# Hybrid decoder trunk: the first half of x loaded in three pieces, the norm weights first, fewer idle turns

## The chip, the cores and the metric

The kernel runs on one core of a Trainium2 chip. The metric is the device time of one execution in microseconds (us); lower is better. Times are medians of several executions.

## The reference

Two layers of a decoder trunk on 256 tokens of width 1024, in float32. Each layer computes:

```python
h = rms_norm(x, g_mix[l])
parts = split(h @ w_in[l])                  # one projection, 10656 columns
# A: sliding-window attention, B: latent attention, C: dilated attention in 3 groups,
# M: cross-attention into rms_norm(mem)
y = einsum('bsnc,ncd->bsnd', o, w_branch[l])
x = x + einsum('bsnd,de->bse', sigmoid(gate_pre + b_gate[l]) * y, w_out[l])
u = rms_norm(x, g_mlp[l]) @ w_up[l]
x = x + square(relu(u)) @ w_down[l]
```

## The kernel before, in words

All products are made in three passes of float32r: each operand is split in a rounded part ("hi") and the rest ("lo"), and TensorE adds hi x hi, hi x lo and lo x hi (L1524 to L1526). 200 MB of weights are streamed once. SyncE (SP) walks the list of weight units in order (L929): a unit is one or two blocks of 128 rows by 512 columns, in a ring of four places, `raw`. Before it issues unit u it waits until unit u-4 has been split, that is until VectorE has made its lo part (`lo_split`). ScalarE (ACT) makes the hi part of a unit (L1043), VectorE (DVE) the lo part (L1230), and TensorE then does the unit's "chunks", six matmuls for each block of 128 rows.

The activations need a preparation. x lies with the tokens on the partitions and has to be turned: TensorE transposes a block of 128 columns for both token tiles (a "turn", L1555, two transposes a column block), ACT evicts it from PSUM with the column's norm weight as scale into `h_hi` (L1126), DVE makes `h_lo` (L1379). The norm weights `g_mix` of layer 0 come by their own small DMA, are turned by TensorE (`gains_first`, L1493) and kept by ACT (`keep_first`, L1031); the evictions wait for them. A first product needs unit 0's lo part and the `h_lo` of column block 0.

The order on every engine is made in Python before the program is written. `plan` makes a list of items with modelled costs, needs, an `order` number and sometimes an earliest time `since`. `arrange` places them: again and again it takes the engine that can begin soonest, and on it, among the items that can begin within a small look-ahead (0.1 us on TensorE, 0.25 on ACT and DVE, none for DMA), the one with the lowest order. For DMA items it adds up modelled transfer times from 2.2 us on at 300 GB/s; an item that needs a transfer becomes ready 1.2 us after it. The item `gains_first` has `since=4.0`. The costs are 0.276 us for a turn of one block, 0.15 for `gains_first`, 0.25 for `keep_first`, 0.49 for an eviction of one block, and 0.62 and 0.69 for a one-block unit's hi and lo part. The order numbers at the start are -9.0, -7.64, -6.28, -4.92 for units 0 to 3 (loads, hi and lo), -20 to -17 for the turns of column blocks 0 to 3, three less for their evictions, and 0 for `gains_first` and `keep_first`.

The real transfers are written by hand beside that. SP issues units 0 to 4, then after unit 4 the positions and the rotary frequencies (L934, L936; many descriptors of 4 and 192 bytes), then unit 5 and behind it the second half of x (L932). ACT issues columns 0 to 255 of x (L1021), the norm weights (L1022) and columns 256 to 511 (L1023), and then begins its list. `mem` is loaded by ACT after the hi part of unit 5.

TensorE begins with 14 idle turns of the identity (L1478), has 8 more ahead of the first chunk, and otherwise follows the plan. The first squares of x (`square`) wait for all pieces of x.

Of the kernel before, what the change touches and what calls it, by code (L numbers as in the profile page):

```python
# [7 lines left out]
P = 128  # L8
# [11 lines left out]
DC = D // P  # L20
# [31 lines left out]
MASK = {("A", 0): (0, P), ("A", 1): (P, S), ("B", 0): (0, P), ("B", 1): (P + S, S),  # L52
        ("C", 0): (P + 2 * S, C_BLOCKS * P), ("C", 1): (P + 2 * S + C_BLOCKS * P, C_BLOCKS * P)}
MASK_W = P + 2 * S + 2 * C_BLOCKS * P
STAT = {"h": ("h", 0), "y": ("r", 0), "lat": ("r", 0), "lat3": ("r", 3), "m": ("r", 0), "r0": ("r", 0), "r1": ("r", 4)}
LOADS = 7
ALL_LOADS = 9 * DEPTH - 1
# [95 lines left out]
def plan():  # L153
# [8 lines left out]
    def item(kind, engine, cost, needs, order=None, chain=None, since=0.0, **a):  # L162
        it = Item(kind, engine, cost, axis[0] if order is None else order,
                  [b if isinstance(b, tuple) else (b, None) for b in needs if b is not None], a, since)
        chain = kind if chain is None else chain
        if chain:
            if chain in last_of:
                it.needs.append((last_of[chain], None))
            last_of[chain] = it
        items.append(it)  # L170
        return it
# [325 lines left out]
    masks = item("masks", "DVE", 2.0, [], order=15.0, since=15.4)  # L497
    selects = item("selects", "POOL", 5.0, [masks], order=25.0)

    for k, (size, order) in enumerate(((256, -8.95), (256, -7.6), (512, -0.7))):  # L500
        x_loads.append(item("load_x", "DMA", 256 * size * 4 / 300e3, [], order=order, part=k))
    gains_first = item("gains_first", "PE", 0.15, [], since=4.0)
    gains_first = item("keep_first", "ACT", 0.25, [gains_first])
    gains_turn = item("gains_turn", "PE", 0.15, [], since=20.0, order=20.0)
# [5 lines left out]
    for l in range(DEPTH):  # L510

        def x_turns(c0, c1, dest, gain, came, jobs_needed, order=None):
            for c, m in [(c, 1) for c in range(c0, half)] * (not jobs_needed) + [(c, 2) for c in range(max(c0, 0 if jobs_needed else half), c1, 2)]:
                turn(("x", jobs_needed), came if jobs_needed else [(x_loads[min(c // 2, 2)], 1.2)], c, m, P, dest, "split", gain, l,
                     order=order if jobs_needed or c >= half else c - 20.0)

        if l == 0:
# [197 lines left out]
def hybrid_block(nc, x, mem, positions, inv_freq, g_mix, w_in, b_gate, a_qn, a_kn, a_sink, b_qa_norm, b_kva_norm,  # L715
# [34 lines left out]
    with ExitStack() as ctx:  # L750
# [3 lines left out]
        def sem(name):  # L754
            return ctx.enter_context(nc.semaphore(name))
# [103 lines left out]
        bias_landed = [sem("bias_landed%d" % i) for i in range(2)]  # L859
        mem_landed = [sem("mem_landed%d" % i) for i in range(TT)]  # L860
        gains_landed = sem("gains_landed")
        x_landed, freq_landed = [sem("x_landed%d" % i) for i in range(3)], sem("freq_landed")
        seeded = sem("seeded")
        pool_const, dve_const, ident_ready = sem("pool_const"), sem("dve_const"), sem("ident_ready")
        angle_ready, trig_ready, table_ready = sem("angle_ready"), sem("trig_ready"), sem("table_ready")
# [52 lines left out]

        x_rows = x.rearrange("b (t p) d -> p (b t) d", p=P)

        @block.sync
        def _(sp):
            at_u = {}
            for u, w in enumerate(units):
                if u >= RAW:
                    sp.wait_ge(lo_split, u - RAW + 1)
                l, r0 = w["l"], w["l"] * rows[w["w"]] + w["row"]
                src = flat[w["w"]][r0:r0 + w["kn"] * P, w["col"]:w["col"] + w["cn"]]
                sp.dma_start(unit_in(raw, raw_up, u), src.rearrange("(k p) n -> p k n", p=P))\  # L929
                    .then_inc(raw_landed[u % RAW], 16)  # L930
                if u == 5:
                    sp.dma_start(xs[:, :, NW:D], x_rows[:, :, NW:D]).then_inc(x_landed[2], 16)  # L932
                if u == 4:
                    sp.dma_start(pos_in.bitcast(I32), positions.rearrange("b (t p) -> p (b t)", p=P),  # L934
                                 allow_slow_non_contiguous=True).then_inc(freq_landed, 16)
                    sp.dma_start(inv_in, inv_freq.broadcast_to([P, FREQ])).then_inc(freq_landed, 16)  # L936
                if l == 0 and u >= 9 or l and units[u - 1]["l"] < l:
                    at_u[l] = min(at_u.get(l, u), u)
                if l in at_u:
                    if l and u == at_u[l]:  # L940
                        sp.wait_ge(gain_table, count["table"] // DEPTH * l)
                    for dst, src in row_gains(l)[2 * (u - at_u[l]):2 * (u - at_u[l]) + 2]:
                        sp.dma_start(dst, src.broadcast_to([P, src.shape[1]]), allow_slow_non_contiguous=True).then_inc(gains_landed, 16)
            to = out.rearrange("b (t p) d -> p (b t) d", p=P)
            first, second = jobs[-2], jobs[-1]
            sp.wait_ge(set_free[first.j % 2], set_value(first))
            sp.dma_start(to[:, :, 0:NW], xs[:, :, 0:NW]).then_inc(stored, 16)
            sp.wait_ge(half_added, 1)
            sp.dma_start(to[:, 0, NW:D], xs[:, 0, NW:D]).then_inc(stored, 16)
            sp.wait_ge(set_free[second.j % 2], set_value(second))  # L950
            sp.dma_start(to[:, 1, NW:D], xs[:, 1, NW:D]).then_inc(stored, 16)
            sp.wait_ge(stored, 48)
# [65 lines left out]

        @block.scalar
        def _(act):  # L1020
            act.dma_start(xs[:, :, 0:2 * P], x_rows[:, :, 0:2 * P]).then_inc(x_landed[0], 16)  # L1021
            act.dma_start(g_first, g_mix[0].rearrange("(c p) -> c p", p=P)).then_inc(g_first_landed, 16)  # L1022
            act.dma_start(xs[:, :, 2 * P:NW], x_rows[:, :, 2 * P:NW]).then_inc(x_landed[1], 16)  # L1023
            act.wait_ge(seeded, 1)
            nc.scalar.activation(nothing[:], no_mask[:], ACT.Sin)
            gained = False
            for it in placed["ACT"]:
# [19 lines left out]
                elif it.kind == "square":  # L1047
# [3 lines left out]
                    if src == "D":  # L1051
                        job, seg = a["job"], a["segs"][0]
                        tile = home_of(homes[a["tok"]])
                        act.wait_ge(set_free[job.j % 2], set_value(job))
                        if seg.get("st") == 2 * HD:
                            to = sq[:, 0:TT * seg["n"] * HD].rearrange("p (t h d) -> p t h d", t=TT, d=HD)
                            of = tile[:, :, 0:4 * B_W].rearrange("p t (h d) -> p t h d", d=B_W)[:, :, :, 0:HD]
                        else:
                            w = job.cn
                            if not seg.get("st"):  # L1060
                                w = max(g["col"] + g["n"] * g["d"] for g in a["segs"])
                            to = sq[:, 0:TT * w].rearrange("p (t c) -> p t c", t=TT)
                            of = tile[:, :, 0:w]
                        nc.scalar.activation(to, of, ACT.Square).then_inc(squares, 1)
                    else:
                        if a["q"] >= STATS:
                            act.wait_ge(root_ready, a["q"] - STATS + 1)
                        if src == "x":
                            for c in range(3):
                                act.wait_ge(x_landed[c], 16)  # L1070
                            for job in a["jobs"]:
                                act.wait_ge(set_free[job.j % 2], set_value(job))
                            of = xs[:, a["tt"]]
                        else:
                            act.wait_ge(mem_landed[a["tt"]], 16 * (a["l"] + 1))
                            of = mem_in[:, a["tt"]]
                        nc.scalar.activation(sq[:], of, ACT.Square, accum_out=sums[:, slot, 0:1]).then_inc(squares, 1)
# [396 lines left out]
        def _(pe):  # L1474
            def idle_turns(n):

                for _ in range(n):
                    nc.tensor.transpose(ps_d[:, 1, 0, 0:P], ident[:], ident[:])  # L1478

            pe.wait_ge(ident_ready, 1)  # L1480
            idle_turns(14)
            for it in placed["PE"]:
                a = it.a
                if it is first_chunk:
                    idle_turns(8)
                for b, closes, count_freed in a["prior"]:
                    if closes is not None and closes.kind == "mask":
                        pe.wait_ge(masked, closes.a["e"] + 1)
# [39 lines left out]
                elif it.kind == "turn":  # L1528
                    (src, i), b, m, wd = a["source"], it.banks[0], a["m"], a["width"]
                    if src == "tok":  # L1530
                        if a["ready"] is not None:
                            pe.wait_ge(tok_ready, a["ready"] + 1)
                        else:
                            pe.wait_ge(scaled, a["scaled"] + 1)
                    elif src == "x":
                        if not i:
                            pe.wait_ge(x_landed[min(a["c"] // 2, 2)], 16)
                        for job in i:
                            pe.wait_ge(set_free[job.j % 2], set_value(job))
                        if a["piece"]:  # L1540
                            pe.wait_ge(part_added, a["piece"])
                    elif src == "mem":
                        for tt in range(TT):
                            pe.wait_ge(mem_landed[tt], 16 * (a["l"] + 1))
                    elif src == "Y":
                        pe.wait_ge(y_added, a["mixed"].a["added"])
# [96 lines left out]
```

## Time and profile before

| | us |
|---|---|
| median of 3 runs | 1180.99 (1180.57 to 1181.22) |
| the profiled execution, its own time | 1182.1 |
| its span in the trace | 1180.3 |
| first real product starts (in the span) | 7.39 |
| PE busy | 1174.4 |
| DVE busy | 822.2 |
| ACT busy | 698.0 |

The profile counts time from the start of the span. A busy time of TensorE holds the modelled ends of overlapping matmuls, so in a dense stretch it is the starts of successive matmuls that tell the pace. The change touches only the first microseconds; the rows shown below are from there and from the places that lie behind them.

### The profile page before, as it was taken

Reading aid. Unit: us, or ns where it says so; the run is one execution under the profiler, and the core shown is the slowest. Engines: PE = TensorE matmul, PEld = TensorE weight load, DVE = VectorE, ACT = ScalarE, POOL = GpSimd, SP = SyncE. Lnnn points to the kernel's source line nnn. Section 1 sums busy time; section 2 is a strip of 40 time slices with the busy share of each in tenths; the row PEclk is TensorE's granted clock in tenths of the full one; section 3 lists DMA queues with packets and bytes.
Section 4 is the critical chain, followed back from the end, with each engine's and each line's share of the span. In section 5 each row is a group of like instructions: output and inputs, shape, how many; then the busy total and the mean of one; then the engine's idle time right before and its main releaser. Section 6 shows DMA issues by size and latency. Waiting matters only on the chain.

```text
span 1180.3 us, 18491 instructions
## 1 busy us (share of the span) xinstructions
PE 1174.4 (100%) x6808; PEld 1007.7 (85%) x6808; DVE 822.2 (70%) x1319; ACT 698.0 (59%) x1114; POOL 139.9 (12%) x129
## 2 busy tenths in 40 slices
PE   9999999999999999999999999999999999999998
PEld 7888888888888899999888888888888888999897
DVE  6787989987766764454567788989876767555544
ACT  6667866655544474555476677666654445655453
POOL 6211422300000000000021123232000000000000
PEclk9999999999999999999999999999999999999999
DMA  8655446554576556565756554465545665665653
GB/s 280 197 157 157 127 140 197 160 171 129 163 211 203 182 174 190 186 190 186 205 153 200 145 155 126 140 192 168 161 139 165 179 198 177 179 194 182 194 182 105
DMA packets 127878, 204.75 MB, mean 173 GB/s; under 512 B 9206, under 2 KB 50736, under 8 KB 127792
## 3 DMA queue, kind: packets, MB, share of 16 engines
q1 hardware_dynamic: 122528, 194.64, 54.7%
q10 hardware_dynamic: 4720, 8.92, 2.5%
q8 instruction: 56, 0.92, 0.3%
q14 instruction: 30, 0.25, 0.1%
q0 software_dynamic: 544, 0.03, 0.0%
HBM read 200.41 MB, written 1.05 MB: 171 GB/s over the span
## 4 chain that ended last, share of the span: by engine, by line
PE 95%; DMA 2%; DVE 2%; ACT 1%; POOL 1%; issue 1%; ACTq 0%; POOLq 0%; DVEq 0%
PE ps_d L1524 23%; PE ps_d L1526 22%; PE ps_d L1525 22%; PE ps_b L1515 5%; PE ps_b L1517 5%; PE ps_b L1516 5%; PE ps_b L1579 4%; PE ps_b L1555 3%; PE ps_b L1613 3%; PE ps_b L1587 2%; DMA raw<-in_m_w_kv_dram 1%; DMA raw<-in_w_in_dram 1%; DVE w_lo L1230 1%; PE ps_d L1478 0%; POOL root L984 0%
## 5 line engine op out<-in xcount | busy, mean ns | idle before, releaser
L1230 DVE TENSOR_TENSOR w_lo<-raw,w_hi 128x1024 fp32r<-128x1024 f32 (+3 forms) x382 | 450.6, 1185 | 265.5 <-ACT w_hi L1043 264.2
L1043 ACT ACTIVATE w_hi<-raw 128x1024 fp32r<-128x1024 f32 (+3 forms) x382 | 391.8, 1027 | 371.1 <-PE ps_d L1526 282.1
L1524 PE MATMUL ps_d<-w_hi,h_hi 128*128 128x512 f32 (+3 forms) x704 | 279.5, 397 | 0.0
L1526 PE MATMUL ps_d<-w_hi,h_lo 128*128 128x512 f32 (+3 forms) x704 | 267.3, 380 | 0.0
L1525 PE MATMUL ps_d<-w_lo,h_hi 128*128 128x512 f32 (+3 forms) x704 | 266.9, 379 | 0.0
L1524 PE MATMUL ps_d<-w_hi,r_hi 128*128 128x512 f32 (+1 forms) x552 | 217.5, 394 | 0.0
L1526 PE MATMUL ps_d<-w_hi,r_lo 128*128 128x512 f32 (+1 forms) x552 | 214.1, 388 | 0.0
L1525 PE MATMUL ps_d<-w_lo,r_hi 128*128 128x512 f32 (+1 forms) x552 | 214.0, 388 | 0.0
L1526 PEld LDWEIGHTS ps_d<-w_hi,h_lo 128*128 128x128 f32 x704 | 132.3, 188 | 25.1
L1524 PEld LDWEIGHTS ps_d<-w_hi,h_hi 128*128 128x128 f32 x704 | 132.5, 188 | 24.8 <-issue 2.9
L1525 PEld LDWEIGHTS ps_d<-w_lo,h_hi 128*128 128x128 f32 x704 | 132.8, 189 | 20.5
L1515 PE MATMUL ps_b<-h_hi,w_hi 128*128 128x256 f32 x512 | 145.6, 284 | 0.0
L1517 PE MATMUL ps_b<-h_hi,w_lo 128*128 128x256 f32 x512 | 144.9, 283 | 0.0
L1516 PE MATMUL ps_b<-h_lo,w_hi 128*128 128x256 f32 x512 | 144.9, 283 | 0.0
L1524 PEld LDWEIGHTS ps_d<-w_hi,r_hi 128*128 128x128 f32 x552 | 103.8, 188 | 21.0 <-ACT q_c L1095 0.6
L1526 PEld LDWEIGHTS ps_d<-w_hi,r_lo 128*128 128x128 f32 x552 | 103.6, 188 | 21.0
L1525 PEld LDWEIGHTS ps_d<-w_lo,r_hi 128*128 128x128 f32 x552 | 103.8, 188 | 19.1
L984 POOL TENSOR_TENSOR root<-sums,power 128x16 f32<-128x16 f32 (+3 forms) x32 | 82.4, 2576 | 271.6 <-DVE sums L1308 259.4
L1515 PEld LDWEIGHTS ps_b<-h_hi,w_hi 128*128 128x128 f32 x512 | 98.2, 192 | 1.3 <-issue 0.5
L1516 PEld LDWEIGHTS ps_b<-h_lo,w_hi 128*128 128x128 f32 x512 | 98.3, 192 | 0.5
L1517 PEld LDWEIGHTS ps_b<-h_hi,w_lo 128*128 128x128 f32 x512 | 98.2, 192 | 0.0
L984 POOL TENSOR_TENSOR factor_mlp<-sums,inverse 128x1 f32<-128x1 f32 x4 | 2.2, 558 | 371.7 <-DVE sums L1317 371.7
(172 smaller groups left out, 1158.6 us busy)
## 6 DMA issues: line engine op xcount, KB each, us to landing
raw<-in_w_in_dram SPq DMA_DIRECT2D x150, 512.0 KB, 3.7
raw<-in_w_up_dram SPq DMA_DIRECT2D x64, 512.0 KB, 3.7
raw<-in_w_down_dram SPq DMA_DIRECT2D x64, 512.0 KB, 3.7
raw<-in_w_branch_dram SPq DMA_DIRECT2D x32, 512.0 KB, 3.8
raw<-in_m_w_kv_dram SPq DMA_DIRECT2D x16, 512.0 KB, 5.8
raw<-in_w_out_dram SPq DMA_DIRECT2D x16, 512.0 KB, 4.2
early<-in_b_gate_dram ACTq DMA_DIRECT2D x16, 256.0 KB, 4.2
raw<-in_w_in_dram SPq DMA_DIRECT2D x12, 256.0 KB, 3.5
```

Source lines behind the costliest of these rows:

```text
L984: nc.gpsimd.tensor_tensor(to, sums[:, slot, 0:w], by, ALU.pow).then_inc(root_ready, 1)
L1043: nc.scalar.activation(unit_in(w_hi, hi_up, u), unit_in(raw, raw_up, u), ACT.Copy).then_inc(hi_split, 1)
L1230: nc.vector.tensor_tensor(unit_in(w_lo, lo_up, u), unit_in(raw, raw_up, u), unit_in(w_hi, hi_up, u).bitcast(F32), ALU.subtract).then_inc(l ...
L1515: nc.tensor.matmul(o, wh, hi[:, a["c"]], start=a["first"], stop=False)
L1516: nc.tensor.matmul(o, wh, lo[:, a["c"]], start=False, stop=False)
L1517: last = nc.tensor.matmul(o, wl, hi[:, a["c"]], start=False, stop=a["last"])
L1524: nc.tensor.matmul(o, hi[:, a["c"], cut], wh, start=a["first"], stop=False)
L1525: nc.tensor.matmul(o, hi[:, a["c"], cut], wl, start=False, stop=False)
L1526: last = nc.tensor.matmul(o, lo[:, a["c"], cut], wh, start=False, stop=a["last"])
L1555: last = nc.tensor.transpose(ps_b[0:wd, b, k * P:(k + 1) * P], v, ident[:])
L1579: last = nc.tensor.matmul(ps_b[:, b, c:c + wide], q, k, start=True, stop=True)
L1613: last = nc.tensor.matmul(ps_b[r0:r0 + d, b, c:c + P], v[:, vh * d:(vh + 1) * d], turned_prob_of(st)[:, k * P:(k + 1) * P], start=k == 0, ...
```

## The change

Columns 0 to 511 of x come in three pieces (one column block, one, and two) instead of two of 256 columns. The first of them is issued by ACT, now behind the norm weights; the second and third by SP, behind units 0 and 1. The second half of x stays behind unit 5. Each turn waits for the piece that its block is in; the squares wait for four. The planner gets four x transfers, with orders -9.05, -8.95, -7.6, -0.7. The idle turns go from 14 to 10 at the beginning, and from 8 to 5 ahead of the first chunk.

```diff
+X_LOADS = ((0, 1), (1, 2), (2, 4), (4, DC))
+X_LOAD = [k for k, (c0, c1) in enumerate(X_LOADS) for _ in range(c0, c1)]
...
-    for k, (size, order) in enumerate(((256, -8.95), (256, -7.6), (512, -0.7))):
-        x_loads.append(item("load_x", "DMA", 256 * size * 4 / 300e3, [], order=order, part=k))
+    for k, ((c0, c1), order) in enumerate(zip(X_LOADS, (-9.05, -8.95, -7.6, -0.7))):
+        x_loads.append(item("load_x", "DMA", S * (c1 - c0) * P * 4 / 300e3, [], order=order, part=k))
...
-                turn(("x", jobs_needed), came if jobs_needed else [(x_loads[min(c // 2, 2)], 1.2)], ...
+                turn(("x", jobs_needed), came if jobs_needed else [(x_loads[X_LOAD[c]], 1.2)], ...
...
+        def load_x(eng, k):
+            cut = slice(X_LOADS[k][0] * P, X_LOADS[k][1] * P)
+            eng.dma_start(xs[:, :, cut], x_rows[:, :, cut]).then_inc(x_landed[k], 16)
...
-                if u == 5:
-                    sp.dma_start(xs[:, :, NW:D], x_rows[:, :, NW:D]).then_inc(x_landed[2], 16)
+                if u in (0, 1, 5):
+                    load_x(sp, {0: 1, 1: 2, 5: 3}[u])
...
-            act.dma_start(xs[:, :, 0:2 * P], x_rows[:, :, 0:2 * P]).then_inc(x_landed[0], 16)
             act.dma_start(g_first, g_mix[0].rearrange("(c p) -> c p", p=P)).then_inc(g_first_landed, 16)
-            act.dma_start(xs[:, :, 2 * P:NW], x_rows[:, :, 2 * P:NW]).then_inc(x_landed[1], 16)
+            load_x(act, 0)
...
-            idle_turns(14)
+            idle_turns(10)
...
-                    idle_turns(8)
+                    idle_turns(5)
...
-                            pe.wait_ge(x_landed[min(a["c"] // 2, 2)], 16)
+                            pe.wait_ge(x_landed[X_LOAD[a["c"]]], 16)
```

## Rows read from the trace of the kernel before

**Rows 1.** Busy time by engine, from the page: us, share, instructions.

```profile
PE 1174.4 (100%) x6808; PEld 1007.7 (85%) x6808; DVE 822.2 (70%) x1319; ACT 698.0 (59%) x1114; POOL 139.9 (12%) x129
```

**Rows 2.** Waits of TensorE, whole span: us in total, times, longest.

```profile
PE ps_d L1478 <- POOL ident L962: 1.8, 1, 1.8
PE ps_b L1555 <- DVE tok L1360: 0.8, 1, 0.8
```

**Rows 3.** Timeline, TensorE: start us, length us, engine line operation.

```profile
1.78 3.25 PE L1478 MATMUL ps_d<-ident 128*128 128x128 f32 x14 [1.78 <-POOL ident L962]
...
5.06 0.27 PE L1493 MATMUL ps_d<-ident,early 8*128 8x8 f32 x1
...
5.26 1.11 PE L1555 MATMUL ps_b<-ident,xs 128*128 128x128 f32 x4
...
6.17 1.47 PE L1478 MATMUL ps_d<-ident 128*128 128x128 f32 x8
...
7.39 0.48 PE L1524 MATMUL ps_d<-w_hi,h_hi 128*128 128x512 f32 x1
...
14.55 0.39 PE L1526 MATMUL ps_d<-w_hi,h_lo 128*128 128x512 f32 x1
...
14.94 1.07 PE L1555 MATMUL ps_b<-ident,xs 128*128 128x128 f32 x8
```

**Rows 4.** Timeline, ScalarE, ahead of the first product and at 21 us.

```profile
4.34 0.63 ACT L1043 ACTIVATE w_hi<-raw 128x512 fp32r<-128x512 f32 x1 [0.51 <-DMA raw<-in_w_in_dram]
...
5.37 0.18 ACT L1031 ACTIVATE g_all<-ps_d 128x8 f32<-128x8 f32 x1 [0.40 <-PE ps_d L1493]
...
5.99 0.90 ACT L1126 ACTIVATE h_hi<-ps_b,g_all 128x256 fp32r<-128x256 f32 x2 [0.44 <-PE ps_b L1555]
...
21.65 1.06 ACT L1043 ACTIVATE w_hi<-raw 128x1024 fp32r<-128x1024 f32 x1 [1.89 <-DMA raw<-in_w_in_dram]
```

**Rows 5.** Timeline, VectorE, ahead of the first product.

```profile
5.00 0.69 DVE L1230 TENSOR_TENSOR w_lo<-raw,w_hi 128x512 fp32r<-128x512 f32 x1 [5.00 <-ACT w_hi L1043]
...
6.50 0.91 DVE L1379 SCALAR_TENSOR_TENSOR h_lo<-ps_b,g_all,h_hi 128x256 fp32r<-128x256 f32 x2 [0.80 <-ACT h_hi L1126]
...
7.44 1.29 DVE L1230 TENSOR_TENSOR w_lo<-raw,w_hi 128x512 fp32r<-128x512 f32 x2
```

**Rows 6.** Timeline, DMA issues on the queues of SP and ACT.

```profile
0.74 5.36 SPq L929 DMA_DIRECT2D raw<-in_w_in_dram  x5
0.75 0.48 ACTq L1021 DMA_DIRECT2D xs<-in_x_dram  x1
...
1.26 0.61 ACTq L1022 DMA_DIRECT2D early<-in_g_mix_dram  x1
...
6.66 0.47 SPq L936 DMA_DIRECT2D early<-in_inv_freq_dram  x1
...
8.16 0.37 SPq L929 DMA_DIRECT2D raw<-in_w_in_dram  x1
...
8.57 0.47 SPq L932 DMA_DIRECT2D xs<-in_x_dram  x1
```

**Rows 7.** DMA issues of 0 to 0.9 us: KB, us to landing.

```profile
xs<-in_x_dram ACTq DMA_DIRECT2D x1, 256.0 KB, 4.3
```

**Rows 8.** DMA issues of 8.5 to 9 us.

```profile
xs<-in_x_dram SPq DMA_DIRECT2D x1, 512.0 KB, 6.2
```

**Rows 9.** DMA issues of the whole span, from the page: median us to landing.

```profile
raw<-in_w_in_dram SPq DMA_DIRECT2D x150, 512.0 KB, 3.7
```

**Rows 10.** Busy time by stretch; the last three numbers: granted clock, DMA share, GB/s.

```profile
4.00:5.00 1.00, 1.00 (x5) 0.63 (x3) 0.00 (x0) 0.63 (x1) 1.00 (x3) 1.00 1.07 398
...
9.00:10.00 1.00, 1.00 (x9) 0.87 (x8) 0.21 (x1) 0.72 (x2) 1.00 (x3) 1.00 0.27 45
...
12.00:14.00 2.00, 2.00 (x10) 1.65 (x10) 0.85 (x1) 0.56 (x1) 0.18 (x1) 1.00 1.06 400
```

**Rows 11.** The chain that ended last, in order of time: start us, us, what.

```profile
12.88 8.75 DMA raw<-in_w_in_dram
```

More of the change, by code:

```diff
@@ L513, in x_turns @@
             for c, m in [(c, 1) for c in range(c0, half)] * (not jobs_needed) + [(c, 2) for c in range(max(c0, 0 if jobs_needed else half), c1, 2)]:
-                turn(("x", jobs_needed), came if jobs_needed else [(x_loads[min(c // 2, 2)], 1.2)], c, m, P, dest, "split", gain, l,
+                turn(("x", jobs_needed), came if jobs_needed else [(x_loads[X_LOAD[c]], 1.2)], c, m, P, dest, "split", gain, l,
                      order=order if jobs_needed or c >= half else c - 20.0)
@@ L861, in hybrid_block @@
         gains_landed = sem("gains_landed")
-        x_landed, freq_landed = [sem("x_landed%d" % i) for i in range(3)], sem("freq_landed")
+        x_landed, freq_landed = [sem("x_landed%d" % i) for i in range(len(X_LOADS))], sem("freq_landed")
         seeded = sem("seeded")
@@ L1068, in _ @@
                         if src == "x":
-                            for c in range(3):
-                                act.wait_ge(x_landed[c], 16)
+                            for landed in x_landed:
+                                act.wait_ge(landed, 16)
                             for job in a["jobs"]:
```

## The prediction

> **What bounds the kernel now.** I read four views, in this order. The page's busy times: TensorE is busy for 1174.4 of the 1180.3 us of the span [rows 1], so the end moves only by what TensorE does more or less, or waits more or less. TensorE's waits: beside the wait for the identity there is one named stall, 0.8 us, for a rotated token tile [rows 2]; it lies at 62.5 to 63.7 us. The timeline of the first 15 us: real work starts at 7.39 and is dense up to 14.55, where the turns of the second half of x follow at 14.94 instead of about 0.23 later; that is a small stall of 0.16 us, and x's second half, issued at 8.57, lands 6.2 us after, at 14.8 [rows 3, 6, 8]. The chain that ended last: it does not run over the first product alone but, from 12.88, over a weight transfer of 8.75 us [rows 11], which ACT awaited for 1.89 us up to 21.65 [rows 4], and from there over ACT and DVE work to the stall at 62.5. So two things reach the end: TensorE's own start, less what the stall at 62.5 swallows (up to 0.9 us), and the time at which the transfers after 8 us land. The second is the stronger, because it moves the stall itself.
>
> **The order that the planner gives.** I followed its rules with the new numbers; I take only the order from them, not a time. The modelled transfers are: piece 0 to 2.64 us, unit 0 to 3.51 (3.07 before), piece 1 to 3.95, and from unit 1 on as before. Block 0's turn can begin at 3.84, before `gains_first` with its `since` of 4.0, so TensorE now has turn 0, `gains_first`, turn 1. `keep_first` is ready at 4.41 and unit 0's hi part at 4.71, out of the look-ahead of 0.25; then block 0's eviction (4.66, order -23) goes ahead of the hi part too. ACT's order was hi 0, keep, evict 0, evict 1; it becomes keep, evict 0, **hi 0**, evict 1. DVE's was lo 0, h_lo 0, h_lo 1, lo 1; it becomes h_lo 0, lo 0, h_lo 1, lo 1. From unit 2's lo part on the modelled times fall together within 0.03 us, and the rest of the order stays.
>
> **Piece 0 and the norm weights.** The old first piece was issued at 0.75 and landed 4.3 later, at 5.05 [rows 6, 7]; the norm weights were there for the turn at 5.06 [rows 3]. Piece 0 is now issued behind the norm weights, whose issue takes 0.61, so at about 1.37 [rows 6]. Ahead of it stand unit 0 and piece 1, and pieces 0 and 1 together are the 256 KB of the old first piece. I therefore let it land when the old one did plus 0.1 for rows half as long: T = 5.15. Lower bound: half of 256 KB is saved at 398 GB/s [rows 10], 0.33, so 4.7. Upper bound: the old 4.3 from the new issue, 5.7. The norm weights land earlier, but nothing uses that, since their turn now stands behind block 0's.
>
> The Trainium skill ("DMA: Bandwidth & Descriptors", section "Anatomy of one DMA", measured on GpSimd's path) puts a DMA at 2.0 us and its bytes over 436 GB/s; by it 128 KB less would save 0.3 us, and the first product would be late by about 0.2 instead of the 0.5 below. The trace's 4.3 us for 256 KB is far over the 2.6 us of that rule, so it is the transfers ahead, not the size, that this landing waits for.
>
> **From T to the first product.** Two transposes at 0.23 (3.25 us / 14 [rows 3]): 0.46. Norm weights turned and kept: 5.06 to 5.37+0.18 was 0.49 [rows 3, 4]. Eviction of block 0: 0.90 / 2 = 0.45. Hi part of unit 0: 0.63 [rows 4]. Lo part: 0.69 and 0.03 of hand-over [rows 5]. Sum 2.75, so lo 0 ends at 5.15 + 2.75 = 7.90, and it was over at 5.69. The first product starts at 7.9 instead of 7.39: **+0.5 us**. Before, hi 0 and lo 0 lay under the wait for x (4.34 to 5.69); now they are in the line behind it. Bounds from T: +0.1 to +1.1.
>
> **Idle turns.** Ten end at about 1.8 + 2.3 = 4.1, ahead of T. The five behind turn 1 run from about 6.3 to 7.4, under the ACT and DVE work. So the seven that go, 7 x 0.23 = 1.6 us, give 0: the wait behind them is what is late. If they had been in the way they would be worth up to 0.4 (before, `h_lo` of block 0 was ready near 7.0 and the product waited for the idle turns until 7.39 [rows 3, 5]); that is the bound below zero. A cost above zero is the clock rival.
>
> **SP's queue, the main term.** SP issues unit 4 when lo 0 is done. That was 6.10 - 0.38 = 5.72 [rows 5, 6]; it will be 7.95, **+2.2**, and the positions and frequencies behind it are as much later. Unit 5 needs lo 1: 7.90 + h_lo 1 (0.45) + 0.65 = 9.0, but SP itself is busy with the frequencies until 6.66 + 0.47 + 2.2 = 9.35. Unit 5 goes at 9.35 instead of 8.16, and the second half of x at 9.75 instead of 8.57: **+1.2**. The two issues added ahead (pieces 1 and 2, some 0.47 each) push units 1 to 3 by up to 0.9, into time in which the DMA engines have work anyway. With its old 6.2 us the second half of x lands at 16.0. TensorE would be there at 14.94 + 0.5 - 0.16 = 15.3 and waits for it. So everything behind is **1.2 us** later, not 0.5. Unit 4 (about 12.2 with its old flight, hi and lo part 1.06 + 1.23 behind it) would be ready at 14.5, against a TensorE that wants it at about 13.9: 0.6 us, inside the same wait.
>
> Does the rest follow? The DMA engines are full from 12 us on (400 GB/s) and nearly idle between 9 and 10 (45 GB/s) [rows 10]; the full stretch starts with unit 5 and x and has to carry the same bytes, so the unit that ACT awaited until 21.65 is 1.2 later too, and `mem`, which is issued behind unit 5's hi part. The stall at 62.5 then moves with it. Upper bound of the term: the idle dip comes from the frequencies' small descriptors, and these are 2.2 later; if unit 5 keeps its distance from them, the term is 2.2. Lower bound: with less queued ahead unit 5 flies in 3.7 [rows 9] and x's 512 KB follow 1.3 behind it (at 400 GB/s), so x lands at 14.4, no later than before, and the term is 0.
>
> **Sum.** +1.2 us (0 to 2.2). The profiled execution would have 1182.1 + 1.2 = 1183.3 as its own time (span 1181.5). It was 1.1 above the median; on the median the forecast is 1180.99 + 1.2 = **1182.2**. A difference within 0.2% (2.36 us) can't be told from no change here.
>
> **Rivals.**
> Not slower, "x's second half is no later": by the lower bound above, the dip at 9 to 10 us closes and the flight of x is at most 5.0 us. TensorE's 0.3 us delay is swallowed at 62.5. Time 1180.5 to 1181.2. For it: the dip is real idle time. Against it: the descriptors that made it are still ahead of unit 5. It decides from a flight of 5.0 us down.
> Slower, "the frequencies set it": term 2.2, time 1183.2. For it: unit 5 was issued at 8.16 and the engines were still idle between 9 and 10.
> Slower still, "the clock rises later": the idle turns ran at 0.23 us each and the later turns of x at 1.07 / 8 = 0.13 [rows 3], so TensorE left the 1.2 GHz level during the eight idle turns, although the column of the granted clock shows 1.00 there. The new order leaves it without work from 4.1 to 5.15 and from 7.4 to 7.9. If it therefore stays at 1.2 GHz for two chunks (12 products of 0.23 more each) that is 2.8 us, of which the wait for x covers 0.7: 1182.2 + 2.1 = 1184.3. The Trainium skill ("TensorE: Matmul & The Clock Gate", section "What's actually happening") states that the slow clock is the default and activity releases it, at a moment that varies from run to run; it speaks for this rival, and no row here shows a rise after such a gap.
> Faster, "the order stays as it was": if my reading of the planner fails and hi 0 keeps its place, the first product comes up to 0.5 earlier, at 6.9, but the second half of x is not earlier: 1180.6 to 1181.0.
>
> **Chances.** Forecast 0.45, x no later 0.20, frequencies 0.18, clock 0.10, old order 0.07. The forecast's own range is 1181.5 to 1182.9. The range for all, leaving out most of the clock case and the low edge: 1180.1 to 1184.0. Faster by over 0.2% (below 1178.6) fits none of the cases: 0.04 for what I have not seen. Slower by over 0.2% (above 1183.35): most of the clock case and the edge of the frequencies case, 0.13. Within: 0.83.
>
> **What would show it.** In the changed kernel's timeline: TensorE with two turns of x, L1493, two turns; ACT with L1031 and one eviction ahead of the first L1043; the first L1230 ending near 7.9; unit 4 issued near 7.95 and the second half of x near 9.75; its turns near 16.1; the stall at 62.5 still there, and its end near 64.9. I am wrong if the first L1043 still comes first, if x's second half lands before 15 us, or if the products behind the first stand 0.43 apart.

## The result, and the profile after

| | before | changed | |
|---|---|---|---|
| median of 20 runs, us | 1181.04 | 1183.34 | ratio 1.0019 (1.0012 to 1.0026) |
| lowest to highest | 1180.57 to 1181.91 | 1182.40 to 1184.09 | |
| profiled execution, its own time | 1182.10 | 1183.94 | |
| its span | 1180.3 | 1182.1 | +1.8 |
| first product starts | 7.39 | 7.94 | +0.55 |
| turns of the second half of x start | 14.94 | 18.02 | +3.08 |
| stall near 62.5 us | 0.8 named | none | |

The change makes the kernel 2.3 us slower, some 0.19%, and the whole interval lies above 1. The forecast was +1.2, to 1182.2, with an own range of 1181.5 to 1182.9 and a range for all cases up to 1184.0. The ratios here and below leave out two disturbed runs that took far longer, one of the kernel before (1953 us) and one of `a_order` (4144 us).

Timeline of TensorE in the changed kernel (start us, length us), to be held against [rows 3]:

```profile
1.78 2.40 PE L1483 MATMUL ps_d<-ident 128*128 128x128 f32 x10 [1.78 <-POOL ident L968]
4.88 0.69 PE L1560 MATMUL ps_b<-ident,xs 128*128 128x128 f32 x2 [0.70 <-DMA xs<-in_x_dram]
5.50 0.27 PE L1498 MATMUL ps_d<-ident,early 8*128 8x8 f32 x1
5.70 0.69 PE L1560 MATMUL ps_b<-ident,xs 128*128 128x128 f32 x2
6.18 1.27 PE L1483 MATMUL ps_d<-ident 128*128 128x128 f32 x5
7.94 0.76 PE L1529 MATMUL ps_d<-w_hi,h_hi 128*128 128x512 f32 x1 [0.49 <-DVE w_lo L1235]
8.50 0.63 PE L1530 MATMUL ps_d<-w_lo,h_hi 128*128 128x512 f32 x1
8.93 0.63 PE L1531 MATMUL ps_d<-w_hi,h_lo 128*128 128x512 f32 x1
...
11.35 0.39 PE L1530 MATMUL ps_d<-w_lo,h_hi 128*128 128x512 f32 x1
11.58 0.39 PE L1531 MATMUL ps_d<-w_hi,h_lo 128*128 128x512 f32 x1
...
16.36 0.39 PE L1531 MATMUL ps_d<-w_hi,h_lo 128*128 128x512 f32 x1
18.02 1.06 PE L1560 MATMUL ps_b<-ident,xs 128*128 128x128 f32 x8 [1.27 <-DMA xs<-in_x_dram]
```

Three things to see. The first product waits for a lo part of the weights, not for x. The first products start 0.43 apart (8.50, 8.93) and later ones 0.23 (11.35, 11.58): the first is the 1.2 GHz level of TensorE's clock, the second the 2.4 GHz level. And between 16.36 and 18.02 TensorE waits for the second half of x.

ACT, against [rows 4], and VectorE, against [rows 5]:

```profile
5.80 0.18 ACT L1036 ACTIVATE g_all<-ps_d 128x8 f32<-128x8 f32 x1 [2.49 <-PE ps_d L1498]
6.08 0.47 ACT L1131 ACTIVATE h_hi<-ps_b,g_all 128x256 fp32r<-128x256 f32 x1
6.45 0.62 ACT L1048 ACTIVATE w_hi<-raw 128x512 fp32r<-128x512 f32 x1
6.97 0.47 ACT L1131 ACTIVATE h_hi<-ps_b,g_all 128x256 fp32r<-128x256 f32 x1
```

```profile
6.59 0.48 DVE L1384 SCALAR_TENSOR_TENSOR h_lo<-ps_b,g_all,h_hi 128x256 fp32r<-128x256 f32 x1 [6.59 <-ACT h_hi L1131]
7.11 0.69 DVE L1235 TENSOR_TENSOR w_lo<-raw,w_hi 128x512 fp32r<-128x512 f32 x1
7.71 0.48 DVE L1384 SCALAR_TENSOR_TENSOR h_lo<-ps_b,g_all,h_hi 128x256 fp32r<-128x256 f32 x1
```

The hi part of unit 0 (L1048) stands third on ACT, behind the norm weights and one eviction, where it was first, at 4.34. ACT had been idle for 2.49 us before. Unit 0's lo part ends at 7.80 instead of 5.69.

SP's queue, against [rows 6], and the second half of x, against [rows 8]:

```profile
2.64 5.56 SPq L935 DMA_DIRECT2D raw<-in_w_in_dram  x3
8.24 0.47 SPq L940 DMA_DIRECT2D early<-in_positions_dram  x1
8.76 0.47 SPq L942 DMA_DIRECT2D early<-in_inv_freq_dram  x1
9.27 0.43 SPq L935 DMA_DIRECT2D raw<-in_w_in_dram  x1
9.74 0.47 SPq L925 DMA_DIRECT2D xs<-in_x_dram  x1
```

```profile
xs<-in_x_dram SPq DMA_DIRECT2D x1, 512.0 KB, 8.1
```

Unit 4's issue ends at 8.20 instead of 6.10, the second half of x goes at 9.74 instead of 8.57, and it flies 8.1 us instead of 6.2. The waits of TensorE in the whole span, against [rows 2]:

```profile
PE ps_b L1560 <- DMA xs<-in_x_dram: 2.0, 2, 1.3
PE ps_d L1483 <- POOL ident L968: 1.8, 1, 1.8
PE ps_d L1529 <- DVE w_lo L1235: 0.5, 1, 0.5
```

The stall for the rotated tile is gone. In the kernel before it looked like this:

```profile
62.51 0.39 PE L1526 MATMUL ps_d<-w_hi,r_lo 128*128 128x512 f32 x1
63.66 0.41 PE L1555 MATMUL ps_b<-ident,tok 128*128 128x128 f32 x2 [0.77 <-DVE tok L1360]
```

Two starts are 1.15 us apart where 0.23 is usual, so the stall was some 0.92 us. VectorE finished the tile (L1360, now L1365) at 63.51 before and at 64.45 in the changed kernel, 0.94 later; TensorE reached its last matmul ahead of it at 62.51 and at 65.38, 2.87 later, and no longer had to wait. So 3.08 - 0.92 = 2.16 is what should reach the end; the span shows 1.8, the medians 2.3. The profiled execution of the kernel before took 1182.10, 1.06 above its median, and whether a median execution has this stall is not shown.

### The profile page after: what moved, and what is told of

Same layout as the page of the kernel before. It is cut to its first block, busy times and chain, and to the rows that moved or that the text cites. A ratio compares the mean times of both kernels' runs of the same rounds, so it can differ in the third digit from the quotient of the medians.

```text
span 1182.1 us, 18485 instructions
## 1 busy us (share of the span) xinstructions
PE 1174.7 (99%) x6801; PEld 1007.1 (85%) x6801; DVE 823.1 (70%) x1319; ACT 698.0 (59%) x1114; POOL 139.8 (12%) x129
## 3 DMA queue, kind: packets, MB, share of 16 engines
q10 hardware_dynamic: 4448, 8.53, 2.3%
## 4 chain that ended last, share of the span: by engine, by line
PE 98%; DMA 1%; DVE 0%; issue 0%; ACT 0%; ACTq 0%; SPq 0%
PE ps_d L1529 24%; PE ps_d L1531 23%; PE ps_d L1530 23%; PE ps_b L1520 5%; PE ps_b L1521 5%; PE ps_b L1522 5%; PE ps_b L1584 4%; PE ps_b L1560 3%; PE ps_b L1618 3%; PE ps_b L1592 2%; DMA xs<-in_x_dram 1%; DVE w_lo L1235 0%; DVE xs L1467 0%; ACT w_hi L1048 0%; ACTq L1027 0%
## 5 line engine op out<-in xcount | busy, mean ns | idle before, releaser
L1048 ACT ACTIVATE w_hi<-raw 128x1024 fp32r<-128x1024 f32 (+3 forms) x382 | 391.9, 1027 | 371.8 <-PE ps_d L1531 284.0
```

Source lines behind the costliest of these rows:

```text
L1048: nc.scalar.activation(unit_in(w_hi, hi_up, u), unit_in(raw, raw_up, u), ACT.Copy).then_inc(hi_split, 1)
```

## Experiments

Each kernel ran 11 times (the changed one 20) beside 33 (20) runs of the kernel before on the same chip. The differences are against the runs of the kernel before that were made beside each, and the intervals are about 1 us to either side. "Flight" is the time from the issue of a transfer to its landing. The landing of the second half of x is its issue plus its flight, from one profile each.

| run | median less that of before, us | ratio, 95% | first product | x issued, flight, landed |
|---|---|---|---|---|
| before | | | 7.39 | 8.57, 6.2, 14.8 |
| changed | +2.30 | 1.0012 to 1.0026 | 7.94 | 9.74, 8.1, 17.9 |
| b_order | +2.64 | 1.0014 to 1.0032 | 8.12 | 9.92, 7.6, 17.5 |
| a_order | -0.33 | 0.9988 to 1.0007 | 6.16 | 8.05, 6.9, 15.0 |
| a_idle | +2.63 | 1.0015 to 1.0033 | 7.75 | 9.56, 7.3, 16.9 |
| b_idle | +0.74 | 0.9998 to 1.0015 | 7.29 | 8.76, 5.2, 14.0 |
| a_order_idle | -0.22 | 0.9988 to 1.0005 | 7.38 | 8.47, 5.4, 13.9 |
| a_freq | +1.78 | 1.0005 to 1.0022 | 7.50 | 8.80, 6.2, 15.0 |
| b_freq | +1.74 | 1.0006 to 1.0024 | 6.96 | 8.44, 5.0, 13.4 |
| a_order_freq | +1.57 | 1.0003 to 1.0021 | 6.15 | 8.13, 6.5, 14.6 |
| a_nofreq | +1.45 | 1.0000 to 1.0018 | 7.50 | 8.80, 7.3, 16.1 |
| b_nofreq | +0.46 | 0.9992 to 1.0009 | 7.09 | 8.57, 7.0, 15.6 |
| a_order_x4 | +0.86 | 0.9997 to 1.0014 | 6.20 | 5.36, 5.7, 11.1 |
| a_order_act | +1.31 | 1.0002 to 1.0020 | 6.62 | 8.53, 6.0, 14.5 |

**Is it the order?** `b_order` puts the new order into the kernel before and changes nothing else:

```diff
     placed = arrange(items)
+    pe, act, dve = placed["PE"], placed["ACT"], placed["DVE"]
+    pe[0], pe[1] = pe[1], pe[0]
+    act[0], act[1], act[2] = act[1], act[2], act[0]
+    dve[0], dve[1] = dve[1], dve[0]
```

> The kernel before with nothing changed but the order of the first items: TensorE turn 0, norm-weight turn, turn 1; ACT keep, evict 0, hi 0, evict 1; VectorE h_lo 0, lo 0, h_lo 1. Transfers and idle turns as before. Theory 'the order is the cause': lo 0 ends near 7.9 instead of 5.7, unit 4 is issued near 7.9, the second half of x near 9.7, it lands at 16 to 18, and the time is 1182.5 to 1183.5. Rival 'the pieces of x and their place in SP's queue are the cause': the order alone costs under 0.5 us, 1181.0 to 1181.5.

Its timeline of TensorE, queue of SP, and waits of TensorE:

```profile
8.12 0.47 PE L1528 MATMUL ps_d<-w_hi,h_hi 128*128 128x512 f32 x1 [0.67 <-DVE w_lo L1234]
```

```profile
9.92 0.48 SPq L936 DMA_DIRECT2D xs<-in_x_dram  x1
```

```profile
PE ps_b L1559 <- DMA xs<-in_x_dram: 1.7, 1, 1.7
```

The order alone costs +2.64 us, as much as the whole change, with x still in its old pieces, the old idle turns and the first products 0.23 apart. `a_order` takes only the order out of the change:

```diff
-    ... zip(X_LOADS, (-9.05, -8.95, -7.6, -0.7))
+    ... zip(X_LOADS, (-8.96, -8.95, -7.6, -0.7))
```

> The changed kernel with the old order of the first items (the modelled first piece of x has order -8.96, behind unit 0), all else as changed. Theory 'order': hi 0 starts when unit 0 lands (3.7), lo 0 ends near 5.0, unit 4 is issued near 5.1, the first product near 6.8, the second half of x lands by 14.8; time 1180.5 to 1181.2, as before or a little under, since the second half of x gates TensorE near 14.9. Rival 'pieces and queue': stays at 1183.0 to 1183.6. Rival 'the clock': the products after the first stand 0.43 apart until the clock rises; with the second half of x early this is no longer covered and costs up to 1.4 us, 1182 to 1182.6.

```profile
6.16 0.49 PE L1529 MATMUL ps_d<-w_hi,h_hi 128*128 128x512 f32 x1
```

```profile
8.05 0.47 SPq L925 DMA_DIRECT2D xs<-in_x_dram  x1
```

```profile
PE ps_b L1560 <- DMA xs<-in_x_dram: 1.2, 1, 1.2
```

The loss is gone (-0.33, not told apart from 0). The first product comes 1.2 us earlier than before, at 6.16. That takes the new loads and the fewer idle turns together: with the new loads and the old turns it starts at 7.38 (`a_order_idle` below), with the old loads and fewer turns at 7.29 (`b_idle`). TensorE then waits 1.2 us for the second half of x, which lands where it always did. The order is shown to be the cause from both sides: 2.6 us put in, 2.6 us taken out. `b_order` swaps items on three engines at once, and no run takes one swap alone. On TensorE the norm weights' turn, behind the turn of block 0, starts at 5.67 instead of 5.06; how the loss divides between this swap and those on ACT and VectorE is open.

**The idle turns and the clock.** `a_idle` is the changed kernel with 14 and 8 turns, `b_idle` the kernel before with 10 and 5, `a_order_idle` the change with the old order and 14 and 8:

```diff
-            idle_turns(10)
+            idle_turns(14)
...
-                    idle_turns(5)
+                    idle_turns(8)
```

> The changed kernel with the old 14 and 8 idle turns, else as changed. Theory 'the idle turns only matter for the clock, and that lies under the wait for x': the clock rises near 7 and the first six products stand 0.23 apart, but the second half of x lands near 17.9 as in the changed kernel, so the time is the same within 0.4 us (1183.0 to 1183.6). Rival 'the clock costs 1.4 us': time 1181.7 to 1182.2.

> The kernel before with 10 and 5 idle turns instead of 14 and 8, nothing else. Theory 'covered': the first product starts near 7.0 instead of 7.39, the second half of x still gates TensorE at 14.9, time 1180.8 to 1181.4. Rival 'fewer turns let the clock stay at 1.2 GHz': the products stand 0.43 apart up to about 10 us and the time is 1182 or more.

> The changed kernel with the old order and with the old 14 and 8 idle turns. Theory 'with the old order the turns are in TensorE's way but the wait for the second half of x covers them': the first product comes 0.5 to 0.7 later than in the run with 10 and 5 turns (6.16), so near 6.8, and the time is the same as there within 0.3 us (1180.5 to 1181.2). Rival 'each idle turn ahead of the product is paid': 1181.4 to 1181.9.

First products of `a_idle`, then of `b_idle`:

```profile
7.75 0.47 PE L1529 MATMUL ps_d<-w_hi,h_hi 128*128 128x512 f32 x1 [0.93 <-DVE w_lo L1235]
8.05 0.40 PE L1530 MATMUL ps_d<-w_lo,h_hi 128*128 128x512 f32 x1
8.29 0.39 PE L1531 MATMUL ps_d<-w_hi,h_lo 128*128 128x512 f32 x1
```

```profile
7.29 0.78 PE L1524 MATMUL ps_d<-w_hi,h_hi 128*128 128x512 f32 x1
7.86 0.63 PE L1525 MATMUL ps_d<-w_lo,h_hi 128*128 128x512 f32 x1
8.29 0.63 PE L1526 MATMUL ps_d<-w_hi,h_lo 128*128 128x512 f32 x1
```

With 14 and 8 turns the changed kernel has its first products at 2.4 GHz, 1.2 us are saved in the first chunk (from the first product to the next turns 1.46 us instead of 2.70), and the time is no better (+2.63 against +2.30). TensorE waits 1.7 us for x instead of 1.3; in this one profile x also landed 1.0 earlier, at 16.9. So no cost of the clock is seen in the changed kernel, as the first theory said, though the two intervals leave room for one of up to about 1 us. In `b_idle` the first chunk is "cold", at the 1.2 GHz level throughout, and the median is 0.7 higher; the interval holds 1, so whether fewer turns cost the kernel before anything is not settled. In its profile TensorE reaches the turns of x at 16.13, 1.19 later than before, and x is there; the stall at 62.5 is gone, so most of that lateness is given back. `a_order_idle` comes at -0.22 with a first product at 7.38; the earlier start of `a_order` buys 0.1 us over it, nothing that can be told. In the profile of `a_order_idle` TensorE has no named wait behind the one for the identity:

```profile
PE ps_d L1483 <- POOL ident L968: 1.8, 1, 1.8
```

**The flight of the second half of x.** Its issue moved by 1.17 us, its flight by 1.9. The suspicion was the small descriptors of positions and frequencies, queued 2.1 us later. `a_freq`, `b_freq` and `a_order_freq` put them behind unit 6; `a_nofreq` and `b_nofreq` leave these two transfers out (constants in their place, the rotary tables are not the reference's):

```diff
-                if u == 4:
+                if u == 6:
                     sp.dma_start(pos_in.bitcast(I32), ...
```

> The changed kernel with its own order, but positions and frequencies issued behind unit 6 instead of unit 4, so not ahead of unit 5 and the second half of x. Theory 'the many small descriptors hold up what is behind them': unit 5 goes near 8.8, x near 9.2, and x lands by 14.5 (flight 5.3 instead of 8.1); TensorE then comes to the turns near 16.6 (cold first chunk) instead of waiting to 18.0: time 1181.6 to 1182.2. Rival 'x is late for its issue alone, the flight stays 8': x lands near 17.3, time 1182.6 to 1183.4.

> The kernel before with positions and frequencies issued behind unit 6 instead of unit 4. Theory 'small descriptors hold up unit 5 and x': x is issued at 8.57 as before or earlier and lands near 13.5 to 14 instead of 14.8, the 0.16 us stall at 14.55 goes, little else: 1180.6 to 1181.3. Rival 'the later frequencies delay the angle tables and the chain to the stall at 62.5': 1181.6 to 1182.5.

> The changed kernel with the old order of the first items, and positions and frequencies issued behind unit 6. In the run with the old order alone the first product came at 6.16 and TensorE waited 1.36 us at 13.7 for the second half of x (landing 14.93). Theory 'two gates': x now lands near 13.3 and this wait goes, but the later stall near 62 to 65 us (VectorE's rotated tile), whose chain runs over ACT and VectorE and not over TensorE, comes back by what TensorE gains: time 1180.2 to 1181.2. Rival 'TensorE's own start is the bound': the 1.4 us are all gained, 1179.3 to 1179.8.

> The changed kernel without the two transfers of positions and frequencies: GpSimd writes constants in their place (so the rotary tables are not the reference's). Theory 'order plus small descriptors': x's second half flies 5 to 6 us instead of 8.1 and lands near 14.5 to 15, behind SP only the late lo 0; TensorE comes to its turns near 16.5 with the cold first chunk: time 1181.3 to 1182.1, and what stays over the same edit of the kernel before is the price of the order and the clock alone. Rival 'the descriptors do not matter for the flight': 1183 or more.

> The kernel before without the two transfers of positions and frequencies (constants instead, the tables are not the reference's). Theory 'the small descriptors empty the DMA engines at 9 to 10.5 us': unit 5 lands near 12 and x near 13.3, the 0.16 us at 14.55 and the stall at 62.5 (0.93 us) go: 1179.7 to 1180.4. Rival 'before did not pay for them': 1180.8 to 1181.4.

Waits of TensorE in `a_freq`, `b_freq` and `a_order_freq`:

```profile
PE ps_d L1529 <- DVE w_lo L1235: 0.8, 2, 0.5
PE ps_b L1560 <- DVE tok L1365: 0.6, 1, 0.6
PE ps_b L1560 <- DMA xs<-in_x_dram: 0.3, 1, 0.3
```

```profile
PE ps_d L1524 <- DVE w_lo L1230: 2.2, 2, 1.4
```

```profile
PE ps_d L1529 <- DVE w_lo L1235: 1.1, 1, 1.1
```

The flights shorten as expected where the small transfers go behind (8.1 to 6.2, 6.2 to 5.0), but the time does not follow: `a_freq` is 0.5 better than the changed kernel, which the intervals do not tell from nothing, and in the kernel before, the move makes it 1.74 slower. The wait changes its name. It is now for lo parts of weights (in `b_freq` 1.4 us of it at 23.7 us), whose transfers stand behind the small ones; in `a_freq` and `a_order_freq` the stall for the rotated tile near 64 us is back too. The times are 1182.9, 1183.1 and 1182.9. The first lies in the range of its rival, though not for the rival's reason (the flight did not stay at 8); the other two lie above both of their ranges. Without the two transfers the stretch from 11 to 13 us carries 250 GB/s where the changed kernel, in its two halves, has 37 and 50:

```profile
11.00:13.00 2.00, 2.00 (x10) 1.67 (x9) 1.32 (x2) 1.07 (x1) 1.29 (x3) 1.00 0.84 250
```

```profile
11.00:12.00 1.00, 1.00 (x7) 0.87 (x6) 0.39 (x1) 0.90 (x3) 1.00 (x3) 1.00 0.32 37
12.00:13.00 1.00, 1.00 (x6) 0.79 (x5) 0.99 (x3) 1.00 (x2) 0.19 (x1) 1.00 0.38 50
```

(The first is `a_nofreq`, the second the changed kernel; the last three numbers are granted clock, DMA share, GB/s.) So this dip in the transfers is theirs. It also moves with them: issued from 6.14 it lies at 9 to 11 us (45 and 123 GB/s, kernel before), from 8.24 at 11 to 13 (changed), from 9.47 at 14 to 16 (113 and 136, `b_freq`). Not all of the dip that I saw before is theirs, though. `b_nofreq` still has 96 GB/s at 9 to 10 us, and over two microseconds:

```profile
9.00:11.00 2.00, 2.00 (x11) 1.65 (x10) 1.47 (x3) 1.99 (x4) 2.00 (x5) 1.00 0.87 197
```

And in the kernel before, leaving them out gains nothing (+0.46, interval holds 1; x lands at 15.6, later than with them), against an expected gain of some 1 us; `a_nofreq` is 0.9 better than the changed kernel, less than expected. Without the small transfers the whole change costs 1.45 - 0.46 = 1.0 us; with them 2.3. With intervals of about 1 us on each, that difference is not clear of the noise, and `a_nofreq` has a warm first chunk besides. In the seven profiles with the small transfers right behind unit 4 the flights are 8.1, 7.6 and 7.3 with the new order and 6.2, 6.9, 5.2 and 5.4 with the old: longer by 1.7 on average. That the flight is longer behind the new order is seen in all three. Without the small transfers the two flights are 7.3 and 7.0, nearly alike, which speaks for them as the reason; that 7.0 is longer than the 6.2 with them speaks against it. Each landing is from one profile and varies by over 1 us, and I leave it open.

**Versions that might beat both.** Both start from `a_order`. `a_order_x4` issues the second half of x behind unit 4, ahead of the small transfers; `a_order_act` has ACT issue the small transfers behind its first piece of x:

```diff
-                if u in (0, 1, 5):
-                    load_x(sp, {0: 1, 1: 2, 5: 3}[u])
+                if u in (0, 1, 4):
+                    load_x(sp, {0: 1, 1: 2, 4: 3}[u])
```

> The changed kernel with the old order of the first items, and the second half of x issued directly behind unit 4, ahead of positions and frequencies. Theory 'with the order mended only the second half of x holds the earlier start back': x lands near 10 to 11, the first product comes near 6.2 and TensorE does not wait at 13.5; unit 5 (landing near 14) is in time; the stall near 62 may come back. Time 1179.8 to 1180.8, faster than the kernel before. Rival 'the descriptors then hold up the units instead': a stall of 1 to 2 us for a lo part between 16 and 31 us, as in the runs with the frequencies behind unit 6, time 1182 to 1183.

> The changed kernel with the old order of the first items, and positions and frequencies issued by ACT right behind the first piece of x, at 1.8 to 2.8 us. Theory 'the descriptors cost least where TensorE has not begun': units 2 and 3 land up to 1.5 us later, which the first chunks feel, but the dip at 9 to 11 us is gone, x lands near 13.5, time 1180.0 to 1181.5. Rival 'they hold up units 1 to 3 by more than 2 us': TensorE stalls behind the first chunk, 1182 or more.

Waits of TensorE in `a_order_x4`; a product of `a_order_act`:

```profile
PE ps_d L1529 <- DVE w_lo L1235: 0.9, 1, 0.9
PE ps_d L1529 <- DVE h_lo L1384: 0.6, 1, 0.6
```

```profile
6.62 0.78 PE L1528 MATMUL ps_d<-w_hi,h_hi 128*128 128x512 f32 x1
```

Neither is faster. In the first x lands at 11.1, in time, and what is behind it pays: 0.9 us for a unit's lo part at 17.4 and 0.6 for an `h_lo` at 21.0. That is the rival's mechanism in its smaller half; the time, 1181.9, lies just under the rival's range. The second takes 1182.35 (+1.31), in its rival's range of 1182 or more, but not by the rival's stall: TensorE's only named wait behind the one for the identity is 0.4 us for x at 4.8. Its first chunk is at the 1.2 GHz level, with six products until 9.3. No version of these runs is faster than the kernel before by more than its interval.

## Why the prediction was right, and where a term was off

The direction and the mechanism came out: a new order, a late unit 4, a late second half of x. The number is partly luck. 1183.34 lies above the forecast's own range (1181.5 to 1182.9), inside only the range for all cases, and two of its terms missed in opposite directions.

- **The planner's order**: right in every item, on the three engines, and with it the cause. The 1.3 us of ACT's and VectorE's work on unit 0 (4.34 to 5.69 before) had lain under the wait for x and came behind it: with what follows from that, the order was the whole loss (`b_order`).
- **Landing of piece 0**: forecast 5.15; the turn started at 4.88 and the flight was 3.5 from its issue at 1.37. 0.27 earlier, inside the bounds. In the nine profiles with this load the flight was 2.9 to 3.5, where the forecast had 3.8, and in `a_freq` the turn, at 4.44, came before the lower bound of 4.7.
- **From T to the first product**: forecast 2.75 to the end of lo 0, measured 7.80 - 4.88 = 2.92. First product forecast 7.9, measured 7.94.
- **Idle turns at 0**: right. The seven turns lay under waits, and putting them back does not help (`a_idle`).
- **SP's queue**: unit 4 forecast 7.95, its three issues ended at 8.20 less 0.4, so 7.8; x forecast 9.75, measured 9.74.
- **Flight of x, the term that was mis-sized**: "with its old 6.2 us" it was to land at 16.0; it flew 8.1 and landed at 17.9. The term was 3.1 at the turns of x instead of 1.2. It went over the upper bound of 2.2 as well, which only let the distance to the frequencies stay the same. Its lower bound failed too: x landed at 17.9 and not at 14.4.
- **"The stall at 62.5 then moves with it"**: wrong. It vanished. The unit that ACT awaited until 21.65 came at 24.24, 2.6 later and not 1.2, but the rotated tile only 0.94 later, against TensorE's 2.87; 0.92 us came back. The two errors have opposite signs, and the sum, +2.16 by steps against a forecast of +1.2, stayed inside the range by that luck: +3.08 alone would have been 1184.1. Its likeliest value was 1.1 under the measured one.
- **Rival "the frequencies set it"**: its 1183.2 is the nearest number to 1183.34, and the dip did move with the small transfers. But its sum is not what happened: x was issued 1.2 later and flew 1.9 longer, 3.1 in all, and the stall gave 0.9 back. How much of the 1.9 is the small transfers' is open.
- **Clock rival**: by the sign that the prediction had named, products 0.43 apart, part of it came in, for one chunk and not two (six products 0.20 longer, not 0.23, until 10.6). Its reason was not borne out: the new order's gaps alone did not bring it (`b_order` and `a_idle` are warm), and `b_idle` has it in the old order. What the cold profiles share is the 10 and 5 turns, which are cold in some profiles and not in others. No price of it can be told at the end, against a forecast of 2.1, since x came later than I had assumed. The rule of the Trainium skill ("TensorE: Matmul & The Clock Gate", section "What's actually happening") that activity releases the clock at a moment that varies fits: with 10 and 5 turns the first chunk was wholly cold in the changed kernel and `b_idle`, but warm in `a_order` and `a_nofreq`; with 14 and 8 it was warm in all six profiles.
- **"The order stays as it was"**: it did not, but `a_order` shows what it would have given. The first product was earlier by 1.2 where I had said up to 0.5, the time by 0.3 (not told from 0): 1180.8, inside that rival's 1180.6 to 1181.0.

## What to carry to other kernels

When a list scheduler writes the order by modelled arrival times, an arrival that moves by a fraction of a microsecond can swap two items of a queue that is worked off in order; work out the new order by hand and ask what the item that now waits had been hidden under. A gate that is opened by the work (here a unit's lo part frees the ring for the next transfers) carries the delay to other transfers, and not by the same amount. Here an earlier first product was worth nothing that could be told, since the next gate, the second half of x, stood where it had stood.

## What the runs showed of the hardware that I had not expected

The flight of the same 512 KB transfer of x was between 5.0 and 8.1 us in these profiles, all but one issued between 8.0 and 10.0 us; only part of it follows the edits. With 25 KB in small descriptors left out, the stretch of 11 to 13 us in the changed kernel carried 250 GB/s instead of some 44; leaving them out still did not make the kernel before faster. And the profile's column of the granted clock (the third number from the end) shows 1.00 in the changed kernel's stretch with products 0.43 apart, so in these profiles the spacing of equal matmuls at the start of the span has to be read for the level:

```profile
9.00:10.00 1.00, 1.00 (x4) 0.81 (x3) 0.39 (x1) 0.00 (x0) 1.00 (x3) 1.00 0.84 221
```
